# Small constants on two queues, and the first rows turned by products with a diagonal, in a one-core decoder step

## The reference, cut to what matters

```
h = _rmsnorm(x, norm_mix)          # x * rsqrt(mean(x*x) + EPS) * norm_mix
z = h @ w_in                       # 1024 x 6144
a_b, a_c, a_h, b_val, b_gate, q, g = jnp.split(z, cuts, axis=-1)
conv_a, new_buf_a = _causal_dwconv(buf_a, a_c * a_h, w_conv_a)                    # width 3
conv_b, new_buf_b = _causal_dwconv(buf_b, b_val * jax.nn.sigmoid(b_gate), w_conv_b)  # width 31
y_b = jax.nn.silu(_layernorm(conv_b + b_conv_b, ln_g, ln_b)) @ w_out_b
```

## Time and profile before

| | us |
|---|---|
| median of 3 runs | 1373.85 (1370.41 to 1378.36) |
| the profiled execution's own time | 1369.97 |
| its span, first to last instruction | 1368.2 |
| first transpose of x | 7.79 |
| first product of the projection | 13.39 |
| PE busy over the span | 1272.8 (93%) |
| DVE, ACT, POOL busy | 451.1, 239.9, 117.0 |

### The profile page before, as it was taken

The page is one execution under the profiler, slowest core; times in us unless marked ns, Lnnn a source line. Parts: engine busy times, 40 slices in busy tenths (PEclk is TensorE's granted clock), DMA queues, the critical chain, the costliest instruction groups (busy, mean ns, idle before and its releaser), DMA issues.

```text
span 1368.2 us, 14526 instructions
## 1 busy us (share of the span) xinstructions
PE 1272.8 (93%) x5975; PEld 579.7 (42%) x5975; DVE 451.1 (33%) x800; ACT 239.9 (18%) x345; POOL 117.0 (9%) x152
## 2 busy tenths in 40 slices
PE   7999999999999999999999999999987877887886
PEld 5756766766463333333333333333322222322231
DVE  2897312211363422222222314222422222233235
ACT  4112433310121111111111111111111111111112
POOL 1110100000001010000000000100011000000010
PEclk9999999999999999999999999999999999999998
DMA  9615624362799999999999999999999999999994
GB/s 330 253 62 193 238 102 186 123 246 100 269 370 399 428 424 426 425 427 425 425 426 426 428 425 426 426 426 424 425 425 425 424 426 426 425 427 426 424 390 149
DMA packets 64661, 480.64 MB, mean 351 GB/s; under 512 B 10937, under 2 KB 13113, under 8 KB 39865
## 3 DMA queue, kind: packets, MB, share of 16 engines
q1 hardware_dynamic: 51903, 460.67, 81.6%
q0 software_dynamic: 10672, 15.39, 3.2%
q10 hardware_dynamic: 1994, 3.25, 0.7%
HBM read 478.52 MB, written 22.61 MB: 366 GB/s over the span
## 4 chain that ended last, share of the span: by engine, by line
PE 68%; DMA 29%; DVE 1%; issue 1%; ACT 0%; SPq 0%; POOL 0%; DVEq 0%; ACTq 0%
PE PS L1772 26%; PE PS L1392 15%; DMA ring<-in_w_gu 13%; PE PS L1805 12%; DMA ring<-in_w_dn 10%; PE PS L1334 4%; PE PS L1589 4%; DMA ring<-y_rows 3%; PE PS L1634 3%; DMA arena<-in_w_dn 2%; PE PS L1428 2%; DMA ring<-in_w_in 1%; DMA ring<-in_cache_mem_v 1%; PE PS L1677 0%; DVE XX L1315 0%
## 5 line engine op out<-in xcount | busy, mean ns | idle before, releaser
L1772 PE MATMUL PS<-ring,arena 128*64 128x512 f32 x1824 | 406.0, 597 | 35.6 <-DMA ring<-in_w_gu 28.9
L1245 DVE TENSOR_TENSOR arena<-PS,XX 128x1024 f32<-128x1024 f32 x32 | 39.2, 1225 | 658.5 <-PE PS L1772 658.5
L1772 PEld LDWEIGHTS PS<-ring,arena 128*64 128x64 f32 x1824 | 131.5, 139 | 288.2 <-issue 284.8
L1805 PE MATMUL PS<-ring,arena 128*64 128x512 f32 x896 | 202.3, 600 | 18.3 <-DMA ring<-in_w_dn 17.4
L1392 PE MATMUL PS<-arena,ring 128*128 128x320 f32 x768 | 213.5, 434 | 0.9 <-DMA ring<-in_w_in 0.9
L1392 PEld LDWEIGHTS PS<-arena,ring 128*128 128x128 f32 x768 | 144.1, 190 | 59.4 <-issue 2.0
L1772 PE MATMUL PS<-arena 128*64 128x512 f32 x608 | 136.2, 595 | 14.4 <-DMA arena<-in_w_gu 13.9
L859 ACT ACTIVATE arena<-arena 128x1024 f32<-128x1024 f32 x32 | 33.9, 1058 | 617.8 <-DVE arena L1248 617.8
L540 POOL DMA_INDIRECT y_rows<-arena x60 | 59.7, 995 | 789.4 <-ACT arena L840 753.8
L1805 PEld LDWEIGHTS PS<-ring,arena 128*64 128x64 f32 x896 | 61.8, 137 | 142.3 <-issue 142.2
L1334 PEld LDWEIGHTS PS<-ident,arena 128*128 128x128 f32 (+4 forms) x596 | 64.1, 141 | 53.9 <-issue 49.5
(11 more groups left out here) (206 smaller groups left out, 680.2 us busy)
## 6 DMA issues: line engine op xcount, KB each, us to landing
ring<-in_w_gu SPq DMA_DIRECT2D x96, 2048.0 KB, 27.7
ring<-in_w_dn SPq DMA_DIRECT2D x48, 2048.0 KB, 28.9
arena<-in_w_gu SPq DMA_DIRECT2D x31, 2048.0 KB, 28.1
arena<-in_w_dn SPq DMA_DIRECT2D x16, 2048.0 KB, 30.4
ring<-in_w_in SPq DMA_DIRECT2D x11, 2048.0 KB, 12.5
ring<-in_w_mem_kv SPq DMA_DIRECT2D x2, 2048.0 KB, 20.1
ring<-in_cache_mem_k SPq DMA_DIRECT2D x4, 1024.0 KB, 13.3
ring<-in_cache_mem_v SPq DMA_DIRECT2D x4, 1024.0 KB, 14.9
```

Of the source, the lines that this page charges most:

```text
L1245: nc.vector.tensor_tensor(gbuf[:], PS[:, 0:2, :], g_bias, ALU.add).then_inc(main["g_added"], 1)
L1772: last = mm(PS[64 * h:64 * h + 64, 2 * g + b, :], in_block(xT[:, k, :], b), (spare[kk] if m == BONUS else moe_ring(m, 2)[:, kk]) [:, g * D ...
L1805: last = mm(PS[64 * h:64 * h + 64, 4 + b, :], actT[:, b, j, c * BLK:(c + 1) * BLK], moe_ring(m, 4)[:, j, h * 512:(h + 1) * 512], start=c = ...
```

## The change

Three things. The 31 rows of `w_conv_b` are loaded by two transfers, of 16 and of 15 rows. Of the other small constants all but `norm_mix` are issued by POOL, after its opening fills, on two new semaphores; the waits are split to match. DVE no longer multiplies the x tile by its reciprocal norms: it multiplies the identity by them, which gives a diagonal matrix, and PE turns the raw x tile by a product with this diagonal, in place of the transpose.

```diff
+        pool.dma_start(rowsW[WA:WA + CA, :], a["w_conv_a"][0]).then_inc(pool_in, 16)
+        pool.dma_start(rowsW[BB:BB + 1, :], a["b_conv_b"]).then_inc(pool_in, 16)
+        pool.dma_start(rowsW[LG:LG + 1, :], a["ln_conv_b_g"]).then_inc(pool_in, 16)
+        pool.dma_start(rowsW[LB:LB + 1, :], a["ln_conv_b_b"]).then_inc(pool_in, 16)
+        pool.dma_start(nmem[:], a["norm_mem"][0].rearrange("(p k) -> p k", p=P)).then_inc(pool_in, 16)
+        pool.dma_start(wr[:], a["w_router"][0].rearrange("(p k) e -> p k e", p=P)).then_inc(router_in, 16)
+        pool.dma_start(nffn[:], a["norm_ffn"][0].rearrange("(p k) -> p k", p=P)).then_inc(router_in, 16)
+        pool.dma_start(br[:], a["b_router"].partition_broadcast(P)).then_inc(router_in, 16)
...
-        pool.wait_ge(small_in, 16 * 9)
+        pool.wait_ge(router_in, 16 * 3)
...
-        act.dma_start(nmem[:], a["norm_mem"][0].rearrange("(p k) -> p k", p=P)).then_inc(small_in, 16)
-        act.dma_start(rowsW[0:CB, :], a["w_conv_b"][0]).then_inc(small_in, 16)
...
+        for lo, hi in ((0, 16), (16, CB)):
+            act.dma_start(rowsW[lo:hi, :], a["w_conv_b"][0, lo:hi]).then_inc(small_in, 16)
...
         def mem_turned(ks):
-            act.wait_ge(small_in, 16 * 9)
+            act.wait_ge(pool_in, 16 * 5)
...
-            nc.vector.tensor_scalar(XN[0:r, tt, :], X[0:r, tt, :], rstd[0:r, tt:tt + 1], None, ALU.mult) \
+            nc.vector.tensor_scalar(XN[0:r, tt, 0:r], ident[0:r, 0:r], rstd[0:r, tt:tt + 1], None, ALU.mult) \
                 .then_inc(x_normed, 1)
...
+        dve.wait_ge(consts, 3)
         norm_x(0)
...
-                last = tr(PS[:, 2 * tt + k // 4, c:c + r], XN[0:r, tt, k:D:KT])
+                last = mm(PS[:, 2 * tt + k // 4, c:c + r], X[0:r, tt, k:D:KT], XN[0:r, tt, 0:r], start=True, stop=True)
...
         def turn_states():
-            pe.wait_ge(small_in, 16 * 9)
+            pe.wait_ge(small_in, 16 * 2)
+            pe.wait_ge(pool_in, 16 * 5)
```

More of the change, by code:

```diff
@@ L257, in program @@
     xt_read_high, first_moved = sem("xt_read_high"), sem("first_moved")
+    pool_in, router_in = sem("pool_in"), sem("router_in")
     st_in_done, st_in_read = sem("st_in_done"), sem("st_in_read")
@@ L628, in _ @@
             last.then_inc(xt_read_high, 1)
-        act.dma_start(wr[:], a["w_router"][0].rearrange("(p k) e -> p k e", p=P)).then_inc(small_in, 16)
-        act.dma_start(nffn[:], a["norm_ffn"][0].rearrange("(p k) -> p k", p=P)).then_inc(small_in, 16)
-        act.dma_start(br[:], a["b_router"].partition_broadcast(P)).then_inc(small_in, 16)
         act.dma_start(stA[0:NS * PADA, :], a["state_conv_a"][0].rearrange("s r c -> (s r) c")).then_inc(state_in, 16)
```

## The result

| | before | changed |
|---|---|---|
| median of 22 runs, us | 1371.69 (1369.58 to 1379.39) | 1379.38 (1376.54 to 1383.98) |
| ratio, 95% interval | | 1.0052 (1.0040 to 1.0064) |
| span of the profiled execution | 1368.2 | 1375.9 |

The changed kernel is slower by half a per cent, 7.7 us by either row. The prediction was +0.7 us and a range of 1370.0 to 1378.5, and gave 6 in 100 to a loss of this size. With 22 runs the median of before is 2.2 us under the one that the prediction started from; measured from there the miss is the larger.

A forecast was written before the change was run, and what follows sets the result against it. The chain through PE's first projection product was taken as the bound; the x branch moves it from 13.39 to 14.1, +0.7 us, the earlier weights worth nothing: 1374.5 us as median, range 1370.0 to 1378.5.

The forecast's parts named there:

- What bounds the kernel: Chain of waits from PE's first projection product at 13.39: every microsecond there counts as one at the end.
- Both signs of being wrong: Projection starting before 13.2 or after 15.3; time changing by over 7 us.
- The transfers: Opening loads: with w_conv_b in 16 and 15 rows, the first half weight chunk lands at about 10.0, not 13.26.
- the far bound: POOL's fifth constant transfer, before the states' transposes: lands between 17.7 and 43.1; near end taken, so no wait.
- Rival 3: PE waits at the states' transposes for POOL's transfers: 11.5 us, 1386.0; 4 in 100.
- ACT and DVE: Opening x branch: first square at 4.5, identity scaling 0.2 us, PE's start at 6.6 instead of 7.79.
- one step: PE's x products in the opening: 0.428 us each at the lower clock level, 0.224 at the upper; PE ends at 14.1.
- when does the level rise: PE's clock during the x products: rise between 10.0 and 12.2, so PE ends between 13.6 and 14.6.
- Rival 2: Clock level rises only after the x tiles: PE ends at 15.2, +1.8 us, 1375.7; 16 in 100.

The follow-up runs named there:

- the run with the filling work: Kernel before with constants moved as in the changed kernel, transposes kept, plus dummy PE products while it waits for x: 1370.74 us, ratio 0.9991 (0.9967 to 1.0016).

## Why the prediction was wrong

What bounds the kernel: right. The shift went to the end nearly one for one; PE stands 7.0 us later at the states' transposes, and the medians differ by 7.7. Both signs of being wrong that the prediction had named came: a projection after 15.3, and over 7 us of change.

The transfers: right in the mechanism, too hopeful in size. The half chunk landed at 11.4 (10.7 with the split alone) for an estimate of 10.0 and 13.26 before. That GpSimd's constants would be in time was right: 12.7, where the far bound was 43, and the states' transposes followed chunk "val" without a wait. Rival 3 did not happen.

ACT and DVE: right within 0.2 us each, 0.34 in their sum. First square 4.69 for 4.5, diagonal 0.28 for 0.2, PE's first product 6.94 for 6.6. The second tile's later landing, 7.1 us in the changed kernel, was not foreseen; it cost nothing, because PE was behind.

PE: here it failed, at one step: "At the lower level I take the transpose's 0.214 for a record of the same 128 columns, so 0.428 a product", with 0.224 at the upper. That products are two records, that this speaks against the change, and that the x branch would become the bound were right. But the rows for the upper level, L1677 and L1692, have weights that lie side by side, and the loop at L1347 takes every eighth column. That stride costs 0.24 a record at either level: 0.48 a product, 11.83 us in all for the forecast's 7.5. With the 0.34 of the later start this is the whole way from the forecast's 14.1 to 18.7. I had matched shape and type of the nearest row, and not how its operand lies in memory. Transposes with the same stride had stood in the same table at 0.110, which made the stride look harmless; for a product it is not. Those rows are the memory's, and not "the same transposes later" as the prediction has it, but the transposes of x cost the same at the upper level: 0.11 apart in the run with the filling work. The neighbouring-columns run puts 4.17 us on this alone, and its projection, from 14.61, starts at the edge of the forecast's 13.6 to 14.6: without the stride the rest of the step held.

The clock: "when does the level rise" was the wrong worry. With the stride the products cost the same at both levels, so nothing was saved by its rise, which came at 12.07, inside the forecast's 10.0 to 12.2. Instead the level fell again, at 18.90, and the first 3.6 us of the projection were slow, which made chunk "val" 1.7 us longer. No rival had a fall after the rise. The fall came in the three kernels with a stride of four or eight, during the products or just behind them, and in none of the other six in their first 40 us; no run kept the stride and changed only how densely PE works, so why it comes stays open. How much of the 7.7 us of the medians is the clock's is not shown either: two kernels with transposes, the constants moved and the split alone, had a first chunk as long, 19.59 and 19.33 us, by a late rise in the one execution that was profiled, and their medians are those of the kernel before.

Rival 2 named the right side with a wrong cause and a bound, 15.2, that was no bound: it rested on the same row.

## What to carry to other kernels

When a row stands in for an operation that the trace does not show, match how the operands lie in memory as well as their shape: at the upper level of the clock a float32 product whose weights step by four or eight numbers costs twice one with neighbouring weights, though a transpose of the same columns does not. Before trading a vector instruction that other work hides for more records on the engine that leads to the next stage, count these records at their worst known price. And look at the granted clock of the next stage too: part of the bill may stand there. Where the list of levels has no entry yet, go by the spacing of the records, and don't read a shift of a microsecond or two from one execution of each kernel.

## What the runs showed of the hardware

Weights of a float32 product by stride in numbers, time between records of 128 columns at the upper level: 0.112 us (1), 0.118 (2), 0.233 (4), 0.238 (8). At the lower level: 0.214 (1), 0.233 (4), 0.24 (8). Transposes at stride 8: 0.110 at the upper level and 0.214 at the lower.

With the 31 rows in one transfer the half chunk lands 10.9 and 11.0 us after its issue (two kernels); as 16 and 15 rows, after 8.3 to 9.2 (seven kernels), so 1.7 to 2.6 us earlier. The Trainium skill (DMA: Bandwidth & Descriptors, the section on why a DMA increments its semaphore by 16) has a rule for the number of engines by which 31 rows use one engine, 16 rows 16 and 15 rows 15. The packets one behind another, and side by side after the split, agree with it; no row names the engine of a packet.

The level of TensorE's clock in the first 40 us, from the list in each packed trace. The last column is the time of the first 64 records of the projection:

| run | first rise | fall, and rise after it | chunk "val", us |
|---|---|---|---|
| before | 12.25 | | 17.46 |
| split alone | 16.97 | | 19.33 |
| constants moved, transposes | 17.27 | | 19.59 |
| the same, with filling work | 7.43 | | 17.49 |
| products, neighbouring columns | 10.98 | | 17.42 |
| products, every second | 9.70 | | 17.42 |
| products, every fourth | 11.10 | 17.92, 21.34 | 18.88 |
| products alone, every eighth | 12.76 | 16.18, 23.00 | 19.33 |
| changed, every eighth | 12.07 | 18.90, 22.31 | 19.12 |

A late rise costs the projection as much as a fall. A record of its 320 columns stands 0.53 us from the next at the lower level and 0.27 at the upper.
